# Sums of squares on four column quarters of the array, and scaling with residual addition over four tiles on VectorE, in a fused transformer kernel

## The reference, cut to what matters

```python
def rmsnorm(x, g):
    return x * rsqrt(mean(x * x, axis=-1) + EPS) * g

h = concatenate([meta, x])
for l in range(2):
    mix = hgrn2_mixer(rmsnorm(h, g[0]), ...) if l == 0 else fox_mixer(rmsnorm(h, g[0]), ...)
    h = h + rmsnorm(mix, g[1])
    ff = conv_ffn(rmsnorm(h, g[2]), ...)
    h = h + rmsnorm(ff, g[3])
```

## Time and profile before

| | |
|---|---|
| median of 3 runs | 3407.08 us (3406.38 to 3408.67) |
| span of the profiled execution, the one time the profile gives for it | 3404.4 us |
| busy: PE, DVE, ACT, POOL | 99%, 74%, 51%, 4% |
| lines of `squares_of` (L1328) | 64 float32 products, two records each |

### The profile page before, as it was taken

One profiled execution on the slowest core, in us unless ns is written; L12 is line 12 of the kernel. 1 busy time (PEld: TensorE's weight loads), 2 busy tenths in 40 slices (PEclk: granted clock), 3 DMA queues, 4 the chain that ended last, 5 costly groups with the idle time before them and its releaser, 6 DMA issues. The chain is left out here.

```text
span 3404.4 us, 65711 instructions
## 1 busy us (share of the span) xinstructions
PE 3369.6 (99%) x25119; PEld 3147.0 (92%) x25119; DVE 2516.7 (74%) x3690; ACT 1725.8 (51%) x2638; POOL 124.3 (4%) x116
## 2 busy tenths in 40 slices
PE   9999999999999999999999999999999999999998
PEld 8998899989998989898899889999999998799987
DVE  6886888887887778787788865557786367777863
ACT  4563655545554545455545545446555344555552
POOL 0100202000200100000001000000000000000000
PEclk9999999999999999999999999999999999999999
DMA  4333223332233322222233321212223221123232
GB/s 142 111 105 112 88 88 104 111 111 94 99 105 111 105 79 84 78 83 92 69 104 105 113 99 63 72 59 69 100 92 106 93 77 39 43 75 100 94 104 81
DMA packets 89676, 311.33 MB, mean 91 GB/s; under 512 B 10816, under 2 KB 15296, under 8 KB 89472
## 3 DMA queue, kind: packets, MB, share of 16 engines
q1 hardware_dynamic: 89056, 307.19, 27.0%
q0 software_dynamic: 416, 1.29, 0.1%
HBM read 306.34 MB, written 2.10 MB: 91 GB/s over the span
## 5 line engine op out<-in xcount | busy, mean ns | idle before, releaser
L896 PE MATMUL ps<-x_hi,w_hi 128*128 128x264 f32 (+2 forms) x1840 | 571.9, 311 | 2.6 <-ACT pair L2884 0.9
L896 PE MATMUL ps<-x_hi,w_lo 128*128 128x264 f32 (+2 forms) x1840 | 562.1, 306 | 0.0
L896 PE MATMUL ps<-x_lo,w_hi 128*128 128x264 f32 (+2 forms) x1840 | 561.2, 305 | 0.0
L896 PE MATMUL ps<-h_hi,w_hi 128*128 128x264 f32 (+3 forms) x1282 | 406.8, 317 | 4.3 <-DVE h_lo L3209 1.9
L896 PE MATMUL ps<-h_hi,w_lo 128*128 128x264 f32 (+3 forms) x1282 | 395.8, 309 | 0.0
L896 PE MATMUL ps<-h_lo,w_hi 128*128 128x264 f32 (+3 forms) x1282 | 395.0, 308 | 0.0
L896 PEld LDWEIGHTS ps<-x_hi,w_hi 128*128 128x128 f32 x1840 | 346.4, 188 | 32.0 <-issue 10.2
L896 PEld LDWEIGHTS ps<-x_hi,w_lo 128*128 128x128 f32 x1840 | 347.0, 189 | 14.7
L896 PEld LDWEIGHTS ps<-x_lo,w_hi 128*128 128x128 f32 x1840 | 345.6, 188 | 15.8
L2993 DVE TENSOR_TENSOR w_lo<-raw,w_hi 128x1024 fp32r<-128x1024 f32 x214 | 260.8, 1230 | 107.4 <-ACT w_hi L1843 103.3
L997 PE MATMUL ps<-t_hi,w_hi 128*128 128x256 f32 x1152 | 322.7, 280 | 0.0
(11 more groups left out here) (425 smaller groups left out, 8817.2 us busy)
## 6 DMA issues: line engine op xcount, KB each, us to landing
raw<-wstream SPq DMA_DIRECT2D x577, 512.0 KB, 3.3
res<-xT SPq DMA_DIRECT2D x8, 256.0 KB, 6.7
out<-res SPq DMA_DIRECT2D x8, 256.0 KB, 2.4
near_bias<-consts POOLq DMA_DIRECT2D x1, 512.0 KB, 4.0
g_chunk<-consts POOLq DMA_DIRECT2D x1, 264.0 KB, 3.4
g_keep<-consts POOLq DMA_DIRECT2D x1, 256.0 KB, 3.2
par<-params SPq DMA_DIRECT2D x1, 232.5 KB, 7.5
far_bias<-consts POOLq DMA_DIRECT2D x1, 128.0 KB, 3.5
```

The lines of the kernel that those rows point to most:

```text
L896: m = pe.matmul(ps[:, bank, 0:n], w[:, slot, wt, :], x[:, k, c0:c0 + n], start=first and q == 0, stop=last and q == 2)
```

## The change

It does two things. First, the sums of squares of half 1 at all four seams, and of half 0 at B and D, no longer take eight products on the whole array. Of each block of four tiles every tile gets its own 32 columns of the array and its own 32 partitions of the bank; when both blocks are in, ACT copies the bank times 32 into a free square buffer (`mean_square`) and one product with `mean_w` adds the four quarters (`mean_of`). The square of tiles 4 to 7 now waits for the whole first block. Second, B and D scale and add as C does: gain in ACT's copy, four tiles in one instruction, all on DVE; POOL has no part in it. Places and orders move with this: in half 0 of B and D the blocks stand behind steps 21 and 27 and the mean behind 30; `sums_of` of half 1 comes after tile 5 of the third unit instead of tile 0 of the fourth; in half 1 the first block stands ahead of `x_lo` tile 6 at B and D (before: tile 4) and the rest behind tile 7, at A and C ahead of tiles 0, 2 and 4; the split `lead(3)` and the fourth late tile change places. Semaphores `s_idle` and `s_eps` become one.

```diff
-            add(... "renorm", inputs(*outs), outs=outs, tok=T, lead=4)
+            add(... "renorm", inputs(*outs), halved=1, outs=outs, tok=T, lead=4)
...
+        def in_quarters(st, h):
+            return h == 1 or st["halved"] > 1
...
                 for k in range(KD):
-                    if k == ahead:
-                        for f in between:
-                            f()
-                        between.clear()
+                    if k in between:
+                        between.pop(k)()
                     pe.wait_ge(s_xlo, x0 + k + 1)
...
-                square_steps = (17, 19, 21) if halved == 1 else range(18, 18 + KD)
+                square_steps = {19: 0} if halved == 1 else {21: 0, 27: 1}
...
+                                if h and st.get("outs") and halved > 1 and steps == 30:
+                                    mean_of(st, 0)
...
-                    at1 = (3, 0) if st["kind"] == "project2" else (3, 6) if halved == 1 else (3, 7)
+                    at1 = (2, 5) if st["kind"] == "project2" else (3, 6) if halved == 1 else (3, 7)
...
-                    between.append(lambda: squares_of(st, 1, range(KD)))
+                    first = 0 if halved == 1 else KD - 2
+                    between[first] = lambda: squares_of(st, 1, 0)
+                    between[min(first + 2, KD)] = lambda: squares_of(st, 1, 1)
+                    between[min(first + 4, KD + 1)] = lambda: mean_of(st, 1)
...
+                pe.wait_ge(s_sqr, st["s0"] + KD * h + SQUARES * (block + 1))
+                for j in range(SQUARES):
+                    rows = slice(FG * j, FG * j + FG)
+                    m = pe.matmul(ps[rows, 2 + h, 0:st["tok"] // 2], mean_w[:, rows],
+                                  square_buffer(st, h, SQUARES * block + j), start=block == 0,
+                                  stop=block == KD // SQUARES - 1, skip_group_check=True)
+                m.then_inc(s_sqp, SQUARES)
+            def mean_of(st, h):
+                pe.wait_ge(s_ms, means_of(st, h) + 1)
+                pe.matmul(ps[:, 2 + h, 0:st["tok"] // 2], mean_w[:, :], part_buffer(st, h), start=True, stop=True)\
+                    .then_inc(s_ms, 1)
...
+            def mean_square(st, h):
+                if not in_quarters(st, h):
+                    return s_sqp, st["s0"] + KD * (h + 1)
+                act.wait_ge(s_sqp, st["s0"] + KD * (h + 1))
+                act.activation(part_buffer(st, h), ps[:, 2 + h, 0:st["tok"] // 2], ACT.Copy, scale=float(FG))\
+                    .then_inc(s_ms, 1)
+                return s_ms, means_of(st, h) + 2
...
-                past(act, s_sqp, st["s0"] + KD * h + (k + 1 - SQUARES if k >= SQUARES else 0))
+                past(act, s_sqp, st["s0"] + KD * h + (0 if k < SQUARES else SQUARES if in_quarters(st, h) else k + 1 - SQUARES))
...
-                    for k in range(KD):
-                        normalise(0, k)
-                        if k == 3:
-                            late_tile(0)
+                    scaled(0, 0, KD // 2)
+                    added(0, 0, KD // 2)
+                    late_tile(0)
+                    scaled(0, KD // 2, KD)
+                    added(0, KD // 2, KD)
                     late_tile(1)
...
+                    late_tile(3)
+                    lows(st, 0, (0, 1))
                     lead(3)
-                    lows(st, 0, (0, 1))
-                    late_tile(3)
                     lows(st, 0, (2, 3))
-                    second_half()
+                    by_half(1)
                     lows(st, 0, range(4, KD))
...
-                if st["kind"] == "project2" and not merged(st):
-                    add_mixed(st)
```

More of the change, by code:

```diff
@@ L168, in plan @@
         f0=0,
+        o0=0,
     )
@@ L195, in inputs @@
     def inputs(*outs):
-        return dict(i=1, s=2 * KD, y=2 * KD, x=2 * KD) if outs else {}
+        return dict(i=1, o=2, s=2 * KD, y=2 * KD, x=2 * KD) if outs else {}
     def project2(units, chunks, lead, tok, after, *outs, early=0):
-        down("project2", units, chunks, lead, counts=dict(v=1, a=2 * KD, **inputs(*outs)), after=after, outs=outs,
+        counts = dict(v=1, a=2 * KD, **inputs(*outs))
+        if outs and LATE[len(chunks)] > 1:
+            counts["o"] = 4
+        down("project2", units, chunks, lead, counts=counts, after=after, outs=outs,
              tok=tok, early=early)
@@ L222, in plan @@
     outs = ("norm00",)
-    add("renorm", inputs(*outs), outs=outs, tok=T, lead=4)
+    add("renorm", inputs(*outs), halved=1, outs=outs, tok=T, lead=4)
     add("hgrn", dict(u=4 * KD, t=4 * KD, h=KD))
@@ L636, in square_buffer, with means_of, part_buffer @@
             return (pair[:, 1, :], sums[:, 0, :])[k // 2 % 2][:, half_cols(st["tok"], k % 2)]
-        def merged(st):
-            return st["kind"] == "project2" and st["halved"] == 1
+        def in_quarters(st, h):
+            return h == 1 or st["halved"] > 1
+        def means_of(st, h):
+            return st["o0"] + (2 if h and st["halved"] > 1 else 0)
+        def part_buffer(st, h):
+            return square_buffer(st, h, SQUARES - 1)
         def at_end(i):
@@ L914, in run_idle @@
             def run_idle(n):
-                pe.wait_ge(s_idle, 1)
+                pe.wait_ge(s_set, 1)
                 for _ in range(n):
                     pe.matmul(ps[:, 7, 0:2 * P], idle[:, 0:P], idle[:, :], start=True, stop=True)
-            late, between = [], []
+            late, between = [], {}
             def first_units(st, count, tok):
@@ L938, in first_units @@
                         [(k, j) for k in range(KH, KD) for j in range(4)]
-                ahead = (KD // 2 if st["kind"] == "glu2" else 0) if between else KD
                 hi, lo = x_src
@@ L965, in first_units @@
                         product(0, j, k, w_hi, lo, False, k == KD - 1)
+                for k in sorted(between):
+                    between.pop(k)()
                 if st["t0"]:
@@ L1246, in project @@
                 full = KD - halved
-                steps = squared = 0
-                square_steps = (17, 19, 21) if halved == 1 else range(18, 18 + KD)
+                steps = 0
+                square_steps = {19: 0} if halved == 1 else {21: 0, 27: 1}
                 for n in range(st["early"] if src != (att_hi, att_lo) else 0):
@@ L1285, in project @@
                                 if h and st.get("outs") and steps in square_steps:
-                                    squares_of(st, 0, [squared])
-                                    squared += 1
+                                    squares_of(st, 0, square_steps[steps])
+                                if h and st.get("outs") and halved > 1 and steps == 30:
+                                    mean_of(st, 0)
                             k0 += kn
-                if st.get("outs"):
-                    squares_of(st, 0, range(squared, KD))
+                if st.get("outs") and halved == 1:
+                    squares_of(st, 0, 1)
                 if st.get("scaled") or st.get("outs") and halved > 1:
-                    at1 = (3, 0) if st["kind"] == "project2" else (3, 6) if halved == 1 else (3, 7)
+                    at1 = (2, 5) if st["kind"] == "project2" else (3, 6) if halved == 1 else (3, 7)
                     late.append(lambda j, k: sums_of(st, 1) if (j, k) == at1 else None)
@@ L1322, in sums_of, with squares_of @@
                         .then_inc(s_rst, 1)
[L1324 to L1329, removed]
+            def squares_of(st, h, block):
+                if not in_quarters(st, h):
+                    for k in range(SQUARES * block, SQUARES * (block + 1)):
+                        pe.wait_ge(s_sqr, st["s0"] + KD * h + k + 1)
+                        pe.matmul(ps[:, 2 + h, 0:st["tok"] // 2], mean_w[:, :], square_buffer(st, h, k),
+                                  start=k == 0, stop=k == KD - 1).then_inc(s_sqp, 1)
+                    return
+                pe.wait_ge(s_sqr, st["s0"] + KD * h + SQUARES * (block + 1))
[9 more added lines that the diff above has]
+                    .then_inc(s_ms, 1)
             def renorm(st):
-                squares_of(st, 0, range(SQUARES, KD))
-                between.append(lambda: squares_of(st, 1, range(KD)))
+                squares_of(st, 0, 1)
+                between[0] = lambda: squares_of(st, 1, 0)
+                between[2] = lambda: squares_of(st, 1, 1)
+                between[4] = lambda: mean_of(st, 1)
             def pool_in(st):
@@ L2643, in take @@
                     act.activation(sq, src, ACT.Square).then_inc(s_mixed, 1)
-                    act.activation(dst, src, ACT.Copy, scale=par_of(st["after"], k) if merged(st) else 1.0)\
+                    act.activation(dst, src, ACT.Copy, scale=par_of(st["after"], k))\
                         .then_inc(s_evac if h is None or h == parts(st) - 1 else s_za, 1)
@@ L2714, in project2 @@
                     late_tile(3)
+                    lead(3)
                     roots(tok, other)
@@ L4142, in lead @@
```

43 lines of the change are left out of this document (14 added, 29 removed).

## The result

The changed kernel takes **3413.5 us** (median of 21 runs, 3409.27 to 3416.02) against 3407.15 for the kernel before (21 runs): ratio 1.0018, 95% interval 1.0012 to 1.0024. That is 6.35 us more, where 1.55 were forecast, and above the range. It is just under the 0.2% (6.8 us) that the prediction took as the least that can be told from no change; the interval lies clear of 1 all the same.

The account below looks back on a forecast made before the run. PE bounds the kernel, with its waits for the chain through four engines at the seams (B, D) or its own products (A, C). B and D +1.2, A +0.2, C +0.15: 3407.08 + 1.55 = 3408.6 us, range 3403.5 to 3413.0.

Parts of the forecast that it names:

- Price of a block: PE, sums of squares: four quarter products take 0.60 us together, result after 0.70; one whole float32 product takes 0.44.
- rival 4: Blocks: quarters run one after the other, each block 1.16 us longer; +15.45 us, 3422.5 us; chance 0.06.
- Half 0 of B: Seam B, first half: with blocks and scaling by fours, PE's first product comes 1.0 us sooner, at 2342.4.
- Half 1 of B: Seam B, second half: first block waits behind late `x_lo` tiles, so B ends 0.6 us later; D the same, +1.2 together.
- ACT's 2.4 us of lead: Seam B, second half: sums come sooner, so squares could end at 2355.3 instead of 2357.68; waiting for the block nearly cancels it.
- The seams A and C: Only half 1 changes there: the longer chain takes PE's slack, first product later by 0.2 us at A, 0.15 at C.
- rival 3: Clock falls at B and D in waits around the second block and mean: 3.0 us more, 3411.6 us; chance 0.14.
- Rival 1: Half 1 of B and D: first block comes early enough, each gains 1.5 us; -2.65 us, 3404.4 us; chance 0.14.

Follow-up runs that it names:

- the second profile: Profile of the changed kernel run once more with no edit: span 3412.6 us; the median of those runs is 3414.4 us.
- Experiments 1 and 2: First: kernel before and changed kernel rerun unedited, 3406.98 and 3414.4 us. Second: changed kernel with extra products in PE's waits at B and D, 3409.75 us.
- experiment 4: Changed kernel with half 1's first block at B and D ahead of `x_lo` tile 4 instead of tile 6: 3407.87 us; with filled waits 3407.12.
- part 2 alone: Changed kernel without quarters: eight whole products of squares per half at the places of before, scaling and adding by fours kept; 3402.23 us, 0.9987 to before.
- part 1 alone: Against the kernel before: quarters for half 1 only, first block ahead of `x_lo` tile 4 at B and D, scaling, adding and POOL unchanged; 3419.87 us, ratio 1.0036.
- the control: The kernel before, run again with no edit: 3406.98 us.

## Why the forecast was wrong, step by step

**Price of a block: right as it was defined, too low among other products.** From its start to the next product a block takes 0.58 where 0.60 was worked out; four quarters do run together, so rival 4 is out. But the block starts 0.22 behind the product ahead of it instead of 0.12, and the product behind it is followed after 0.23 instead of 0.12 (rows 2336.96 to 2337.99). So a block puts off the stream of products by 0.79 us, where a whole float32 product, counted in the same way, puts it off by 0.45. Four whole products against a block are 3.0 times by the first count and 2.3 by the second. The Trainium skill (TensorE: Matmul & The Clock Gate, Part 3) has 2.38 times for three column tiles; no run here has three.

**Half 0 of B, "1.0 us ahead": 0.7.** The mean stands 11.14 behind the sum where the working gives 10.9; most of the difference was there by then. Two blocks at 0.79 instead of 0.60 make 0.4, and the 25 steps of products, each a little shorter than 0.37, take some 0.1 of that back.

**Half 1 of B: every wait where it was placed, the sum too small.** PE's wait for `x_lo` tile 4 is 1.32 (forecast about 1.5), squares 4 to 7 come behind the first block, ACT's 2.4 us of lead are lost there. But the root is 1.08 later than before (30.84 behind the sum against 29.76), not 0.6. Counted from the sum, tile 4 of `x_lo` is 0.17 later than worked out, since half 0's lead was smaller; tiles 4 and 5 take 1.17 instead of 1.0; from the block to the first square it is 0.78 instead of 0.70. Two tiles cost more there than eight products of a long stretch, since behind a wait the second product starts 0.20 after the first (2360.73 and 2360.93) and a block stands off from the product ahead of it. The seams A and C cost 0.40 and 0.25 instead of 0.2 and 0.15. At half 1's first product C is 0.15 later, as forecast, and behind a wait of 0.65; A is 0.35 later and without the wait that was expected there, and its waits of 0.87, 0.88 and 1.05 stand ahead of that, around the blocks. How the 0.35 adds up was not worked out. The chains make +2.8 in place of +1.55.

**The step that failed** is the place of the clock in the sum: it stood at nothing there, and as rival 3 it was put at 0.14 with the reason that "each of its waits is shorter than the longest at present". Of the 4.8 us above the forecast 1.25 are the longer chains and some 3.5 the clock. A single wait's length was the wrong measure. The longest wait at present is the one at A, and the clock of 0.50 in the earlier trace rows stands right behind it:

```profile
2029.65 0.53 PE L946 MATMUL ps<-x_hi,w_hi 128*128 128x264 f32 x1 [2.19 <-ACT x_hi L2752]
```

At B no wait of half 1 is over 2.1 us; but in the second profile, in the 5 us ahead of 2363, PE is busy for 2.02, because the waits stand close together with short groups between, and a fall follows. Before, the eight whole products stand there, and no fall follows; at D:

```profile
3036.00:3042.80 6.80, 6.65 (x34) 4.44 (x32) 5.79 (x16) 3.75 (x10) 0.00 (x0) 1.00 0.00 0
```

The pattern was in the rows read for A: 1.67 of 4 us busy, then a clock of 0.50. It makes a fall likely and not certain: in the three profiles with this chain and half 1's waits unfilled (two of the change, one with half 0 filled) a fall follows at D each time and at B twice. The forecast named that row, priced the fall rightly (1.5) and then argued it away. The Trainium skill (TensorE: Matmul & The Clock Gate, "HAM oscillation — how this bites in real kernels") tells of a kernel whose clock drops again with each wait between short bursts. Experiments 1 and 2 agree in that the clock falls behind such waits, at 0.51 to 0.58 over 3 us, and stays up when they are filled. They differ in the waits: there it is one long wait for a transfer each time, 3 to 5 us, and here no single one at B or D is over 2.1 us.

In numbers: 2.8 us of longer chains, shown by the two traces and by the 2.6 that are left with filled waits, and 3.75 us that the fill gives back.

**Rival 1** (the early block) was real as a design, not as a forecast: B gains 0.76 against before where 1.5 was worked out. Squares 4 to 7 end 26.5 behind the sum, as worked out. But in PE's queue the second block stands behind `x_lo` tile 5 and the mean behind tile 7 (2354.99 and 2356.65 in experiment 4), so from the last square to the root it takes 2.5 us instead of 1.75.

## What to carry to other kernels

Products taken off PE are worth nothing where PE would wait for the chain anyway, and they cost if they were what kept its clock up: before removing PE work beside a chain, add up how much work is left between all the waits there, and do not look at the longest wait alone. In an in-order queue a result is as late as the slowest thing placed ahead of it, so a block that frees buffers goes ahead of the first operand that arrives late. When one profiled execution is the fastest of its runs, read the clocks of all runs before trusting a comparison of two traces.

## What the runs showed of the hardware

A fall can come late: at B in the second profile of the change the granted clock was still 1.00 in the first microsecond of full work (2363 to 2364) and only then 0.57. It can also come while PE still waits: at A in part 2 alone the stretch of the wait (2026 to 2030) is at 0.97 already, and PE's first product behind the wait starts at 2030.54. Over most falls the 1 us stretches add up to 1.65 to 1.71 us of lost clock, and over the longer ones, 2029 to 2037 in part 2 alone and 2358 to 2366 in part 1 alone, to 3.41 or 3.42. The same program shows it at different places from one execution to the next: the fall in `hgrn` (2292 to 2298) is in the profiles of before, of the control and of the second run of the change, and not in the first run of the change, where PE's waits there are the same (0.80 and 1.34 us, before 0.80 and 1.35). With 9 or 13 products that no one reads in half 1's waits of a seam, no profile of the three kernels shows a fall at B or D.
